# Computing the second layer's state space tables one block of tokens earlier

## The reference

```
hn = rms_norm(h, norm1_g); proj = hn @ w_in            # 1024 -> 2824
o_a = gated DeltaNet(...)                              # chunked, 4 heads
o_b = s5(...)                                          # 16 groups, 64 complex states each
o_c = differential attention(...)                      # 4 heads
h = h + concat(o_a, o_b, o_c) @ w_out
h = h + peer(rms_norm(h, norm2_g))                     # expert retrieval
```

```
step  = exp(log_step)
a_bar = exp(lam * step)                                # complex
b_bar = ((a_bar - 1) / lam) * B                        # complex
x_t   = a_bar * x_(t-1) + b_bar u_t                    # scan over tokens
y     = Re(C x) + D u
```

```
act = gelu(u_tab[expert] . x);  y = sum_k gate_k * act_k * v_tab[expert_k]
```

## Time and profile before

| | us |
|---|---|
| median of 3 runs | 1678.6 |
| lowest, highest | 1678.04, 1682.74 |
| span of the profiled execution, first to last instruction (the page has no other time of it) | 1676.9 |
| PE busy | 989.6 (59%) |
| DVE busy | 1097.6 (65%) |
| ACT busy | 301.0 (18%) |
| POOL busy | 988.9 (59%) |
| moved by DMA | 628.69 MB, 375 GB/s on the mean |

### The profile page before, as it was taken

One profiled execution on the slowest core, in us unless ns is written; L12 is line 12 of the kernel. 1 busy time (PEld: TensorE's weight loads), 2 busy tenths in 40 slices (PEclk: granted clock), 3 DMA queues, 4 the chain that ended last, 5 costly groups with the idle time before them and its releaser, 6 DMA issues.

```text
span 1676.9 us, 19109 instructions
## 1 busy us (share of the span) xinstructions
PE 989.6 (59%) x5988; PEld 589.1 (35%) x5988; DVE 1097.6 (65%) x2822; ACT 301.0 (18%) x832; POOL 988.9 (59%) x1028
## 2 busy tenths in 40 slices
PE   5887578785653335978674436888763433333334
PEld 5766467452430003655351004665440000000000
DVE  6441499977465798878647666878647767676430
ACT  4433243141100003224110003233110001000000
POOL 0000246677666667646766777556766777777764
PEclk9898779897785657989776567999886655655677
DMA  6323599999999999999999999999999999999997
GB/s 239 116 68 113 170 383 361 419 418 419 419 418 420 419 382 375 419 419 411 417 419 419 419 420 419 419 418 392 415 419 419 420 420 419 419 420 419 420 383 291
DMA packets 172613, 628.69 MB, mean 375 GB/s; under 512 B 19168, under 2 KB 19168, under 8 KB 172512
## 3 DMA queue, kind: packets, MB, share of 16 engines
q0 software_dynamic: 147456, 536.94, 79.3%
q1 hardware_dynamic: 25056, 90.53, 14.1%
HBM read 626.34 MB, written 1.05 MB: 374 GB/s over the span
## 4 chain that ended last, share of the span: by engine, by line
DMA 33%; DVE 21%; PE 16%; issue 14%; POOL 9%; DVEq 3%; ACT 2%; ACTq 0%; POOLq 0%; SPq 0%
DMA uring<-in_u_tab,small 20%; PE ps L414 16%; DMA vring<-in_v_tab,small 13%; DVE uring L1240 10%; POOL vring L1640 5%; POOL uring L1640 4%; DVE sel L1203 1%; DVE sel L1207 1%; DVE small L1211 1%; ACT gd L1325 0%; DVE sa L934 0%; DVE small L1193 0%; DVE small L1161 0%; PE ps L417 0%; DVE small L1172 0%
## 5 line engine op out<-in xcount | busy, mean ns | idle before, releaser
L1240 DVE CUSTOM_DVE_ANT_0 uring<-uring,ps 128x1024 f32<-128x1024 f32 x512 | 619.0, 1217 | 332.9 <-DMA uring<-in_u_tab,small 307.4
L1640 POOL DMA_INDIRECT uring<-in_u_tab,small x512 | 494.7, 966 | 503.3 <-DVEq L1225 198.1
L414 PE MATMUL ps<-vring,wmat 128*32 128x512 f32 x2048 | 393.3, 907 | 548.1 <-DMA vring<-in_v_tab,small 537.3
L1640 POOL DMA_INDIRECT vring<-in_v_tab,small x512 | 494.0, 965 | 167.9 <-issue 139.0
L414 PEld LDWEIGHTS ps<-vring,wmat 128*32 128x32 f32 x2048 | 78.3, 142 | 799.5 <-issue 797.0
L414 PE MATMUL ps<-hnT,wring 128*128 128x128 f32 x1536 | 191.9, 283 | 8.6 <-DMA wring<-in_w_blocks 3.4
L414 PEld LDWEIGHTS ps<-hnT,wring 128*128 128x128 f32 x1536 | 181.6, 197 | 27.5 <-issue 12.7
L414 PE MATMUL ps<-wring,hnT 128*128 128x256 f32 x448 | 111.6, 403 | 1.4 <-ACT hnT L1325 0.7
L414 PEld LDWEIGHTS ps<-wring,hnT 128*128 128x128 f32 x448 | 88.3, 204 | 26.3 <-issue 11.6
L414 PE MATMUL ps<-gd 128*128 128x128 f32 x544 | 72.2, 283 | 20.1 <-ACT gd L1325 20.1
L414 PEld LDWEIGHTS ps<-gd 128*128 128x128 f32 x544 | 67.5, 195 | 40.5 <-ACT gd L1325 24.3
(11 more groups left out here) (276 smaller groups left out, 1093.4 us busy)
## 6 DMA issues: line engine op xcount, KB each, us to landing
wring<-in_w_blocks SPq DMA_DIRECT2D x152, 512.0 KB, 7.1
uring<-in_u_tab,small POOLq DMA_INDIRECT x512, 11.6
vring<-in_v_tab,small POOLq DMA_INDIRECT x512, 11.6
wring<-in_cols SPq DMA_DIRECT2D x4, 512.0 KB, 6.4
sa<-in_rows SPq DMA_DIRECT2D x4, 512.0 KB, 6.4
h<-in_x SPq DMA_DIRECT2D x2, 512.0 KB, 5.2
keysT<-in_keys SPq DMA_DIRECT2D x2, 512.0 KB, 9.4
rows<-in_rows SPq DMA_DIRECT2D x2, 486.0 KB, 8.0
```

Of the source, the lines that this page charges most:

```text
L414: return nc.tensor.matmul(o, a, b, start=start, stop=True, skip_group_check=True)
L1240: V.tensor_tensor_reduce(row_, row_, xp, 1.0, 0.0, ALU.mult, ALU.add, dots[:, j:j + 1]).then_inc(dot_done.sem, 1)
L1640: nc.gpsimd.indirect_dma_start(dst, None, table, bass.IndirectOffsetOnAxis(ap=index, axis=0)).then_inc(done.sem, 16)
```

## The change

The tables of layer 1 are taken out of mix(2) and become generators of their own, next_tables, on DVE and ACT. They are the third part of the Stages that run beside the pairs of block 0, together with mix(1) and attention(1), at slots 76 to 107.6 (DVE) and 75 and 81 (ACT). lambda stays in the mixer, at slots 2 and 29 on DVE and 5 on ACT. The poles (lre, lim, lst) get a small tile of their own and a load of their own, with the s5 output matrices: s5_params, signal s5_in. For layer 1 SP issues both after g2 of block 1 and a wait for gout_done(1), and they land in gd; the scratch is gd too. ACT waits for tables_ready before it writes convm of mix(2). Layer 0's tables keep their place. Computed values are the same.

```diff
@@ signals, loads
-    params_in = signal("params_in", 64)
+    params_in = signal("params_in", 48)
+    s5_in = signal("s5_in", 32)
...
-            sp.dma_start(sa[:, 1024:1536], cols_d[layer, :, HELD_COLS:HELD_COLS + 512]).then_inc(params_in.sem, 16)
...
+        def s5_params(layer):
+            at = COLS["lre"][0]
+            sp.dma_start(poles, cols_d[layer, :, at:at + 3 * MT]).then_inc(s5_in.sem, 16)
+            sp.dma_start(s5_outs(layer), cols_d[layer, :, HELD_COLS:HELD_COLS + 512]).then_inc(s5_in.sem, 16)
...
                     sp.dma_start(g2, rows_d[i // TB, :, HELD_ROWS:NROWS]).then_inc(g2_in.sem, 16)
+                    if i == TB - 1:
+                        sp.wait_ge(*gout_done(i, 1))
+                        s5_params(1)
@@ tiles
-    c_out = sa[:, 1024:1536].rearrange("p (r m c) -> p r m c", r=2, m=MT)
+    def s5_outs(layer):
+        return sa[:, 1024:1536] if layer == 0 else gd[:, 2048:2560]
+    def s5_room(layer):
+        return sa[:, 1536:2560] if layer == 0 else gd[:, 3072:4096]
@@ DVE
-        def tables(i):
+        def lambdas(layer):
+            dve.wait_ge(*params_in(layer, 48))
...
+        def lambda_difference(layer):
...
+        def tables(layer):
+            if layer > 0:
+                dve.wait_ge(*gout_done(TB - 1, 1))
+                dve.wait_ge(*y_done(TB - 1, 4))
+            dve.wait_ge(*s5_in(layer, 32))
             dve.wait_ge(step_ready.sem, layer + 1)
...
             if t == 0:
                 yield place(i, 2)
-                for k in tables(i):
+                lambdas(layer)
+            if i == 0:
+                for k in tables(layer):
                     yield place(i, k)
+            if t == 0:
+                yield place(i, 29)
+                lambda_difference(layer)
...
+        def next_tables():
+            yield 76
+            for k in tables(1):
+                yield 74 + 1.2 * k
...
                 stages = Stages(mix(b + 1), attention(b + 1)) if b + 1 < NI else Stages(final_first())
+                if b == 0:
+                    stages = Stages(mix(1), attention(1), next_tables())
@@ ACT
             elif t == 0:
-                yield place(i, 1)
-                tables_exp(i)
                 yield place(i, 5)
-                tables_sin(i)
+                lambdas(layer)
...
+            if t == 0 and layer > 0:
+                act.wait_ge(tables_ready.sem, layer + 1)
             for part in range(3):
...
+        def next_tables():
+            yield 75
+            tables_exp(1)
+            yield 81
+            tables_sin(1)
```

More of the change, by code:

```diff
@@ L148, in _build @@
     wmat = sb("wmat", [P, 2, 1056])
-    small = sb("small", [P, 1376])
+    small = sb("small", [P, 1408])
     uring = sb("uring", [P, URING, D])
@@ L213, in tiny @@
         sm[0] += n
-        assert sm[0] <= 1376, sm[0]
+        assert sm[0] <= 1408, sm[0]
         return small[:, a:a + n] if dt == F32 else small[:, a:a + n].bitcast(dt)
@@ L246, in _build @@
     jk = tiny(64)
+    poles = tiny(3 * MT)
+    lre, lim, lst = (poles[:, MT * k:MT * k + MT] for k in range(3))
     ps = ctx.enter_context(nc.psum_tensor("ps", [P, 8, 512], F32))
@@ L374, in params @@
             sp.dma_start(cols[:, :], cols_d[layer, :, 0:HELD_COLS]).then_inc(params_in.sem, 16)
-            sp.dma_start(sa[:, 1024:1536], cols_d[layer, :, HELD_COLS:HELD_COLS + 512]).then_inc(params_in.sem, 16)
             sp.dma_start(rows[:, :], rows_d[layer, :, 0:HELD_ROWS]).then_inc(params_in.sem, 16)
             sp.dma_start(keysT[:, :, :].rearrange("p h n -> p (h n)"), keys_d[layer, :, :]).then_inc(params_in.sem, 16)
+        def s5_params(layer):
+            at = COLS["lre"][0]
+            sp.dma_start(poles, cols_d[layer, :, at:at + 3 * MT]).then_inc(s5_in.sem, 16)
+            sp.dma_start(s5_outs(layer), cols_d[layer, :, HELD_COLS:HELD_COLS + 512]).then_inc(s5_in.sem, 16)
         sp.dma_start(h[:, 0, :], x[0, 0:P, :]).then_inc(x_in[0].sem, 16)
         sp.dma_start(cst[:, 0:CST["perm"][0]], cst_d[:, 0:CST["perm"][0]]).then_inc(cst_in.sem, 16)
+        s5_params(0)
         params(0)
@@ L497, in mix @@
             fill(i, "u", 1, M2, True)
-            pe.wait_ge(*params_in(layer, 64))
+            pe.wait_ge(*params_in(layer, 48))
             for k in range(KT):
@@ L793, in add_y @@
             V.tensor_tensor(h[:, t, :], h[:, t, :], yp, ALU.add).then_inc(y_read.sem, 1)
-        def tables(i):
-            layer = i // 2
-            dve.wait_ge(*params_in(layer, 64))
+        def lambdas(layer):
+            dve.wait_ge(*params_in(layer, 48))
             V.tensor_tensor_reduce(jk, row("lq1"), row("lk1"), 1.0, 0.0, ALU.mult, ALU.add, lsum[:, 0:1])
@@ L802, in tables @@
             V.drain().then_inc(lam_sum.sem, 1)
+        def lambda_difference(layer):
+            dve.wait_ge(lam_exp.sem, layer + 1)
+            V.tensor_tensor(nlam, lsum[:, 1:2], lsum[:, 0:1], ALU.subtract)
+            fence()
+            V.tensor_tensor(nlam, nlam, row("laminit"), ALU.subtract)
+        def tables(layer):
[3 more added lines that the diff above has]
+            dve.wait_ge(*s5_in(layer, 32))
             dve.wait_ge(step_ready.sem, layer + 1)
-            V.tensor_tensor(xr, col("lre"), stp, ALU.mult)
-            V.tensor_tensor(th, col("lim"), stp, ALU.mult)
+            V.tensor_tensor(xr, lre, stp, ALU.mult)
+            V.tensor_tensor(th, lim, stp, ALU.mult)
             fence()
@@ L840, in tables @@
             yield 10
-            V.tensor_tensor(t2, col("lre"), col("lre"), ALU.mult)
-            V.tensor_tensor(t1, col("lim"), col("lim"), ALU.mult)
+            V.tensor_tensor(t2, lre, lre, ALU.mult)
+            V.tensor_tensor(t1, lim, lim, ALU.mult)
             fence()
@@ L853, in tables @@
             fence()
[L854 to L857, removed]
+            V.tensor_tensor(kre, are, lre, ALU.mult)
+            V.tensor_tensor(t0, aim, lim, ALU.mult)
+            V.tensor_tensor(kim, aim, lre, ALU.mult)
+            V.tensor_tensor(t1, are, lim, ALU.mult)
             fence()
@@ L865, in tables @@
             V.memset(phase_s[:, :, 0:1], 0.0)
-            dve.wait_ge(lam_exp.sem, layer + 1)
-            V.tensor_tensor(nlam, lsum[:, 1:2], lsum[:, 0:1], ALU.subtract)
+            room = s5_room(layer)
             fence()
-            V.tensor_tensor(nlam, nlam, row("laminit"), ALU.subtract)
             n = 1
@@ L874, in tables @@
                 nc_, ns_ = pw[1] if n in (1, 4, 16, 64) else pw[0]
-                A = sa[:, 1536:2048].rearrange("p (m t) -> p m t", m=MT)[:, :, 0:n]
-                B = sa[:, 2048:2560].rearrange("p (m t) -> p m t", m=MT)[:, :, 0:n]
+                A = room[:, 0:512].rearrange("p (m t) -> p m t", m=MT)[:, :, 0:n]
+                B = room[:, 512:1024].rearrange("p (m t) -> p m t", m=MT)[:, :, 0:n]
                 pcb, psb = bc(pc[:, :, None], [P, MT, n]), bc(psn[:, :, None], [P, MT, n])
@@ L893, in tables @@
             yield 28
+            c_out = s5_outs(layer).rearrange("p (r m c) -> p r m c", r=2, m=MT)
             cre, cim = c_out[:, 0], c_out[:, 1]
             krb, kib = bc(kre[:, :, None], [P, MT, 32]), bc(kim[:, :, None], [P, MT, 32])
-            A, B, A2, B2 = (sa[:, 1536 + k * 256:1792 + k * 256].rearrange("p (m c) -> p m c", m=MT) for k in range(4))
+            A, B, A2, B2 = (room[:, k * 256:k * 256 + 256].rearrange("p (m c) -> p m c", m=MT) for k in range(4))
             V.tensor_tensor(A, cre, krb, ALU.mult)
@@ L1340, in y_copy, with tables_exp, lambdas, tables_sin @@
             copy(s5y[r, :, :], M2[r, 0:256].rearrange("p (c t) -> p c t", c=2)).then_inc(y_ready.sem, 1)
[L1342 to L1347, removed]
+        def tables_exp(layer):
+            act.wait_ge(*s5_in(layer, 32))
+            S.activation(stp, lst, ACT.Exp).then_inc(step_ready.sem, 1)
+        def lambdas(layer):
+            act.wait_ge(lam_sum.sem, layer + 1)
             S.activation(lsum, lsum, ACT.Exp).then_inc(lam_exp.sem, 1)
-            act.wait_ge(half_angle.sem, i // 2 + 1)
+        def tables_sin(layer):
+            act.wait_ge(half_angle.sem, layer + 1)
             S.activation(s2, s2, ACT.Sin)
@@ L1411, in mix @@
             if i == 0:
-                tables_exp(i)
+                tables_exp(layer)
             yield place(i, 35)
@@ L1416, in mix @@
             yield place(i, 37)
-            act.wait_ge(*params_in(layer, 64))
+            act.wait_ge(*params_in(layer, 48))
             for b, o in enumerate((M0, M1)):
@@ L1423, in mix @@
             if i == 0:
-                tables_sin(i)
+                lambdas(layer)
+                tables_sin(layer)
             yield place(i, 40)
```

## The result

The kernel became slower. Its runs took 1712.07 to 1715.8 us, median 1712.88, the kernel before beside it 1679.8: a ratio of 1.0194 [1.0178, 1.021]. Forecast were 1671.1 us, at most 1676.5. The profiled execution took 1712.07 us, its span 1710.2.

What follows compares the result with a forecast made beforehand. The kernel was taken to last its bytes at 419 GB/s plus time the DMA queue is short: 1676.9 - 7.9 + 0.4 + 0 = 1669.4, with 1.7 around the span 1671.1 us; range 1668.5 to 1676.5.

Steps and rivals of the forecast that it cites:

- What bounds the kernel: From about 200 us on, the kernel lasts its bytes at 419 GB/s plus time the DMA engines lack work.
- What is taken away: Block 1, 590 to 650 us: without 31.0 us of DVE work, no loss; gains 7.9 us less 0.4.
- What is added: Block 0, 400 to 500 us: the moved 31 us of DVE work cost 0, ends 0 and 4 us.
- The loads: SP's new wait and two loads: landing at 397.3, DVE asks at 400.4; wait 0, ends 0 and 9 us.
- slower case: Rival at slot 76: a new load lands 19.6 us after issue, DVE stands 9.7 us; 1684.0 us, chance 0.07.
- The sum: Whole run: span 1669.4 us, 1671.1 with 1.7 around it, the gain carried to the end one for one.
- given back later: Rival: dips at 780 to 800 and 1140 to 1200 grow by what block 1 won; 1678.6 us, chance 0.11.

Runs made afterwards that it cites:

- the aligned change: The changed kernel with `small` 1440 floats wide instead of 1408, rings back on a multiple of 256 B: 1677.38 us, 0.998 of the kernel before.
- the kernel without the tables: The changed kernel with `small` 1440, DVE leaving out the second layer's tables and keeping only the signals: 1676.01 us, 0.9975 of the kernel before.

## Why the prediction was wrong, and where it was right

**What bounds the kernel: right, and the error sits in it.** The kernel lasts as long as its bytes at the full rate plus the time that the queue is short. The prediction took the 419 GB/s of the earlier trace rows as belonging to the kernel, whatever is edited, and wrote that "the bytes of after 650 us are the same, so the gain is carried to the end one for one". The bytes are the same (628.69 MB before, 628.71 after). The rate is not. This is the step that failed: the growth of `small` stands in the diff and has no term in the sum. It measured 29.8 us alone (kernel before, padded) and 35.5 between the change and the aligned change (1712.88 - 1677.38, from two sets of runs, with 1679.8 and 1680.08 for the kernel before).

By the count of full rate and losses used above, the 35.5 come to 1389.0 x (419.3/409 - 1) = 35.0 at full rate, less 2.1 of smaller losses, 32.9; the other 2.6 lie behind 1610 us, where the change's last slices run at 353 and 279 GB/s, and were not looked into.

**What is taken away: right.** In the aligned change 590 to 650 runs at the ceiling, DVE waits for gathers there, the queue is 11.1 us deep at 620 to 640 (5.9 before) and 10.1 at 980 to 1000: block 1 does run like block 2. The loss there went from 8.0 to 0.1, forecast 7.9 less 0.4. The first pair of block 1 ends its last gelu at 631.0 us instead of 641.7, 10.7 us earlier.

**What is added: right.** No stretch from 400 to 520 us leaves its ceiling, DVE's waits for gathers in 400:550 fall from 58.0 to 31.0 us in the change and to 30.4 in the aligned change (27 forecast), and the kernel without the tables is not measurably faster. GpSimd asks 3.58 us late at 408.92 in the change, 1.46 after the same dot in the aligned change (2 to 3 forecast), whose longest such wait up to 520 us is 4.36, at 495.62. The queue at 400 to 420 is 14.3 us deep in the aligned change, where a fall to about 10 was forecast.

**The loads: right.** In the change they were issued at 393.44 and 394.15, not at about 390.3, and the exponential came at 401.36, not 397.6; but the mixer on DVE had also come later, at 404.0 instead of 400.4, and DVE lost 0.28 us. At the old rate all of it is early again: in the aligned change the loads go out at 388.55 and 389.25, the exponential comes at 396.54, the mixer ends at 398.7 and DVE's first table operation starts at 399.00. The forecast's slower case, a load 19.6 us under way, did not occur.

**The sum: wrong in its last line too.** Even at the old rate the gain is not carried to the end. 2.7 us of 7.9 arrive; most of the rest is "given back later", a rival that had 0.11. That the later places grow is what the windows show; that they are met in another phase, its mechanism, is not shown, and what was set against it, that weight traffic refills the queue first, did not prevent it. Taken with the ceiling, none of the rivals described this result: the slower one had a late load as its mechanism.

The Trainium skill has a rule near to what was missed. DMA: Bandwidth & Descriptors, How a descriptor splits into AXI transactions, says that a descriptor is cut into transactions of 256 B in beats of 32 B, and that one which doesn't start on a 256 B boundary starts at the boundary below and fetches bytes that nobody uses. As an estimate from that page a row of 4096 B takes 132 beats instead of 128 where it starts 128 B off, 3.1% more, and 130 where it starts 64 B off, 1.6%. The runs agree in kind and roughly in size for 128 B (419.3/409: 2.5%) and not for 64 B, which cost 2.5% as well; and the page speaks of the bytes fetched, while here it is the destination in SBUF that is off. Whether this rule is the cause is therefore open.

## What to carry to other kernels

When a diff resizes a tile, work out where every tile behind it now starts; a ring that indirect gathers fill belongs on a multiple of 256 B, and here 128 B of slack in an unrelated tile of scalars were worth 30 us in 1680. When a whole run shifts by some per cent and the DMA engines' busy share stays where it was, compare the full-rate slices from before the changed code first: a ceiling that moved there isn't a matter of schedule. And a stall removed from one stage of a kernel that its transfers bound is worth what the later dips leave of it (2.7 of 7.9 us here), so forecast the whole row of dips, not the one.

The best version is the change with `small` at 1440: 1677.38 us, 0.998 [0.9971, 0.999] of the kernel before.

## What the runs showed that was not expected

- Gathered rows of 4096 B move at 419 to 420 GB/s when they land on a multiple of 256 B and at 409 when they land 64 or 128 B off one; the DMA engines' share reads 1.03 in both.
- Direct loads of 512 KB into a ring 128 B off cost nothing measurable: 1.0001 [0.999, 1.0011].
- On three of the chips the kernel before took 1845 to 1867 us instead of 1680, and the kernels profiled there show slices of 250 to 375 GB/s. On one of them the same padding cost 1.0016 [0.9988, 1.0043]: a lower ceiling costs little or nothing where something else, not shown here, keeps the rate under it most of the time.
